# The norms' root factor stays in the PSUM bank of the sums

## The reference

```
def rms_norm(x, w):
    xf = x.astype(jnp.float32)
    y = xf * lax.rsqrt(jnp.mean(xf * xf, axis=-1, keepdims=True) + EPS)
    return (y * w.astype(jnp.float32)).astype(x.dtype)
...
for i in range(DEPTH):
    hn = rms_norm(h, norm_mix_pre[i])
    ...                                   # m = the mixer of layer i, on hn
    h = h + rms_norm(m.astype(h.dtype), norm_mix_post[i])
    hn = rms_norm(h, norm_ffn_pre[i])
    f = swiglu_ffn(hn, ffn_w_gate[i], ffn_w_up[i], ffn_w_down[i])
    h = h + rms_norm(f, norm_ffn_post[i])
return h[:, N_META:]
```

## Time and profile before

| What | before |
|---|---|
| median of 3 runs | 3541.22 us |
| lowest and highest run | 3526.09 and 3548.99 us |
| the profiled execution's own time | 3545.44 us |
| its span | 3543.6 us |
| TensorE busy | 3055.1 us, 86% |
| VectorE busy | 1366.1 us, 39% |
| GpSimd busy | 949.4 us, 27% |
| ScalarE busy | 787.8 us, 22% |

### The profile page before, as it was taken

The page is one execution under the profiler, slowest core; times in us unless marked ns, Lnnn a source line. Parts: engine busy times, 40 slices in busy tenths (PEclk is TensorE's granted clock), DMA queues, the critical chain, the costliest instruction groups (busy, mean ns, idle before and its releaser), DMA issues.

```text
span 3543.6 us, 45716 instructions
## 1 busy us (share of the span) xinstructions
PE 3055.1 (86%) x18053; PEld 2867.9 (81%) x18053; DVE 1366.1 (39%) x2269; ACT 787.8 (22%) x1395; POOL 949.4 (27%) x390
## 2 busy tenths in 40 slices
PE   4999877776769899999999876676898999999996
PEld 3999866664548799999999776455897999999995
DVE  2662255544561532322322424765015323223223
ACT  3221143324561310000000431222114100000002
POOL 2443200000003334443543222000423344435430
PEclk8999998876679999999999986555999999999998
DMA  4122300100002221111111242112212211111101
GB/s 158 66 98 88 126 24 27 39 7 20 34 18 68 97 71 47 48 47 36 55 45 42 76 101 50 37 36 42 92 47 84 68 48 47 47 36 59 47 25 64
DMA packets 138917, 201.04 MB, mean 57 GB/s; under 512 B 32208, under 2 KB 108496, under 8 KB 138320
## 3 DMA queue, kind: packets, MB, share of 16 engines
q1 hardware_dynamic: 54544, 113.99, 10.6%
q10 hardware_dynamic: 84288, 85.84, 7.4%
HBM read 153.20 MB, written 46.60 MB: 56 GB/s over the span
## 4 chain that ended last, share of the span: by engine, by line
issue 33%; PE 33%; DVE 13%; POOL 11%; ACT 6%; DMA 3%; ACTq 1%; POOLq 0%; DVEq 0%; SPq 0%
POOL w_hi L486 8%; PE bank L514 5%; PE bank L515 5%; PE bank L516 5%; POOL w_lo L490 3%; PE bank L568 3%; DVE area L1642 2%; PE bank L729 2%; DMA stage<-wstream 2%; DVE area L1565 2%; PE bank L959 1%; PE bank L960 1%; PE bank L721 1%; DVE area L1650 1%; DVE area L1900 1%
## 5 line engine op out<-in xcount | busy, mean ns | idle before, releaser
L514 PE MATMUL bank<-x_hi,w_hi 128*128 128x344 f32 (+2 forms) x3600 | 1166.7, 324 | 60.4 <-DVE x_lo L1588 34.4
L515 PE MATMUL bank<-x_lo,w_hi 128*128 128x344 f32 (+2 forms) x3600 | 1161.2, 323 | 0.0
L516 PE MATMUL bank<-x_hi,w_lo 128*128 128x344 f32 (+2 forms) x3600 | 1156.9, 321 | 0.0
L486 POOL TENSOR_TENSOR w_hi<-stage,const 128x1024 fp32r<-128x1024 f32 x193 | 474.2, 2457 | 2483.7 <-PE bank L516 2463.9
L514 PEld LDWEIGHTS bank<-x_hi,w_hi 128*128 128x128 f32 x3600 | 683.8, 190 | 67.6 <-DVE x_lo L1588 32.7
L515 PEld LDWEIGHTS bank<-x_lo,w_hi 128*128 128x128 f32 x3600 | 682.9, 190 | 1.9
L516 PEld LDWEIGHTS bank<-x_hi,w_lo 128*128 128x128 f32 x3600 | 683.5, 190 | 0.0
L490 POOL TENSOR_TENSOR w_lo<-stage,w_hi 128x1024 fp32r<-128x1024 f32 x193 | 479.2, 2483 | 15.1
L514 PE MATMUL bank<-act_hi,w_hi 128*128 128x344 f32 (+1 forms) x1056 | 347.3, 329 | 31.9 <-DVE area L1945 24.3
L1932 DVE TENSOR_TENSOR area<-area,bank 128x352 f32<-128x352 f32 (+1 forms) x132 | 68.0, 515 | 758.0 <-ACT area L1368 758.0
L516 PE MATMUL bank<-act_hi,w_lo 128*128 128x344 f32 (+1 forms) x1056 | 341.7, 324 | 0.0
(11 more groups left out here) (217 smaller groups left out, 2876.8 us busy)
## 6 DMA issues: line engine op xcount, KB each, us to landing
stage<-wstream SPq DMA_DIRECT2D x193, 512.0 KB, 3.3
proj<-area ACTq DMA_DIRECT2D x28, 520.0 KB, 2.6
area<-proj ACTq DMA_DIRECT2D x40, 256.0 KB, 4.4
resid<-area ACTq DMA_DIRECT2D x6, 1376.0 KB, 5.7
area<-resid ACTq DMA_DIRECT2D x6, 1376.0 KB, 8.6
area<-proj ACTq DMA_DIRECT2D x12, 520.0 KB, 4.3
area<-xT ACTq DMA_DIRECT2D x4, 1376.0 KB, 8.2
resid<-area ACTq DMA_DIRECT2D x3, 1408.0 KB, 6.2
```

Source lines behind the costliest of these rows:

```text
L486: pool.tensor_tensor(per_block(w_hi[:, slot, :]), per_block(stage[:, h, :]), all_ones, ALU.mult).then_inc(high_split, 1)
L514: mm(out[:, 0:n], w_hi[:, slot, wk], hi[:, xk, a:a + n], start=first, stop=False)
L515: mm(out[:, 0:n], w_hi[:, slot, wk], lo[:, xk, a:a + n], start=False, stop=False)
L516: return mm(out[:, 0:n], w_lo[:, slot, wk], hi[:, xk, a:a + n], start=False, stop=last)
```

## The change

Ln and Exp write their result to bank 7, in place over the sums, and VectorE's products read it there as their second tensor input. Since the bank now holds the factor until the products have read it, the sum of an event no longer waits for the Ln of the event before, but for that event's products: nm_normed if it was a pre, nm_resid (the products and the sum onto the residual) if it was a post. The two waits of ScalarE that kept rs apart are gone, and rs is not used any more. The order of the work on each engine stays.

```
+def norm_before(e):
+    at = e - 1
+    if at < 3:
+        return 0, at, 1
+    if at < 21:
+        return 1 + (at - 3) // 6, (at - 3) % 6 // 2, (at - 3) % 2
+    return 4, at - 21, 0
...
                 e = norm_event(r, c, m)
                 if e:
-                    pe.wait_ge(nm_log, e)
+                    r0, c0, m0 = norm_before(e)
+                    pe.wait_ge(*((nm_normed, 3 * r0 + c0 + 1) if m0 else (nm_resid, 3 * (r0 - 1) + c0 + 1)))
...
-                rs = nv["rs"][m][:, 0:n]
-                if m and 3 * r + c:
-                    act.wait_ge(nm_normed, 3 * r + c)
-                elif not m and 3 * (r - 1) + c:
-                    act.wait_ge(nm_resid, 3 * (r - 1) + c)
                 act.wait_ge(nm_sum, e + 1)
-                A(rs, norm_sums[:, 0:n], ACT.Ln, scale=1.0 / D, bias=eps_col).then_inc(nm_log, 1)
+                A(norm_sums[:, 0:n], norm_sums[:, 0:n], ACT.Ln, scale=1.0 / D, bias=eps_col).then_inc(nm_log, 1)
                 act.wait_ge(nm_log, e + 1)
-                A(rs, rs, ACT.Exp, scale=-0.5).then_inc(nm_root, 1)
+                A(norm_sums[:, 0:n], norm_sums[:, 0:n], ACT.Exp, scale=-0.5).then_inc(nm_root, 1)
...
             def norm_scale(r, c, m):
                 dve.wait_ge(nm_root, norm_event(r, c, m) + 1)
-                return nv["rs"][m][:, 0:CUTS[c][1]]
+                return norm_sums[:, 0:CUTS[c][1]]
```

## The result

The changed kernel takes **3492.11 us** (median of 4 runs, 3489.91 to 3492.68), the kernel before 3539.99 us (4 runs, 3526.09 to 3548.99). The ratio is 0.9867, with a 95% interval of 0.9834 to 0.9900: 47 us or 1.3% faster. I had forecast 3517 us, with 3499 as the lower end of the range. The direction was right, and the gain was twice the forecast (47.9 us by the medians against 24.2).

The account below looks back on a forecast made before the run. TensorE, busy 86% of the span, bounds the kernel through its waits and low clock. Terms -15.7 - 11.2 - 4.2 + 2.8 + 4.1 = -24.2 us, against 3541.22, gave 3517 us; range 3499 to 3540.

Parts of the forecast that it names:

- Part 1: At r=1 and r=3, products reading the bank stop waiting for GpSimd: gains of 15.7, 11.2 and 4.2 us.
- rival A: Products, keeping a weight pointer in SBUF, go on losing to GpSimd and both stretches stay: 3548 us, chance 0.12.
- Rival B: The contest with GpSimd moves to the addition at r=1 and r=3, 8 us given back: 3525 us, chance 0.15.
- Part 2: The sum waits for the products: cost 2.8 us at the start, cut 1, and 4.1 us at r=2, cut 2.
- Part 3: Changed lengths of the products, Ln and Exp, and ScalarE's removed waits: each taken as 0.
- rivals C: Reading the bank is slow, priced at 61 ns for each product: 3523 us, chance 0.08.
- D: More gain: the clock holds at r=3 and r=2, products shrink by 63 ns: 3507 us, chance 0.10.

Follow-up runs that it names:

- P and B: The changed kernel with ScalarE's two waits put back ahead of its wait for the sum, the factor staying in the bank: 3512.09 us, ratio 0.9919.
- W: ScalarE's two waits removed; run alone on the kernel before (kept only at the start, cut 1), factor in SBUF: 3513.46 us, ratio 0.9930.
- P alone: The kernel before with only the sum's wait changed, to the products of the event before: 3544.48 us, ratio 1.0022.
- P and W: The changed kernel with Ln and Exp writing the factor to SBUF again and the products reading it there: 3523.69 us, ratio 0.9969.

## Why the prediction was wrong

**Part 1, the bank read: right in kind and in size.** The products no longer wait for GpSimd, so rival A is out, although each keeps its weight pointer in SBUF. At r = 1 the time from the first post products to the sum of (cut 2, post) fell from 1145.10 to 1219.61 = 74.5 us to 1138.24 to 1196.47 = 58.2: 16.3 us against 15.7 forecast. P and B without W has the same 58.2 (1144.83 to 1203.06). At r = 3, where I had 11.2 + 4.2 = 15.4, the same distance fell from 76.3 (2645.17 to 2721.42) to 57.8 us (2618.66 to 2676.44), 18.5. With P and B alone it is 60.1 (2636.43 to 2696.49), so 16.2 are the bank's and 2.3 W's, since table loads lie in that distance too. Two assumptions were too dark. At r = 1 the addition was to lose 2.2 us to GpSimd and lost none: it takes 3.02 us, and the GpSimd instruction that starts with it takes 5.29. At r = 3 it was to lose 1.5 and lost 1.0 (4.00 us in all), since only 1.1 us of a GpSimd instruction were left. And at r = 3 the clock stayed up. Rival B, the contest moving to the addition, did not come: the longest of the 12 additions now takes 3.995 us against 5.175.

**Part 2, the new wait: right alone, cheaper in company.** Alone it cost what the prediction had, 6.9 us forecast and about 8 measured (2 to 13 by the interval). At its two places it was 3.9 us at r = 2 (4.1 forecast) and, from the first Ln to the last products of r = 0, 3.3 us at the start (2.8 forecast). In the changed kernel the sum at r = 2 waits 2.48 us instead of the 3.97 that it waits with P alone, and ScalarE has loaded its table by the time that the sum ends. The rows of TensorE and then of ScalarE:

```profile
2010.72 5.72 PE L579 MATMUL bank<-area,const 128*128 128x344 f32 x13 [2.48 <-DVE area L1586]
```

```profile
2013.22 1.28 ACT L1040 ACT_TABLE_LOAD   x1
2017.35 0.52 ACT L1040 ACTIVATE bank<-bank,sb_eps 128x344 f32<-128x344 f32 x1 [2.85 <-PE bank L579]
```

Post follows pre by 12.9 us (2006.72 to 2019.66): 2.7 us more than before, not 4.1, though the clock fell as forecast (the whole sum takes 6.59 us). At the start the sum begins at 41.60 us, right behind the products that end at 41.55, and the last products of r = 0 begin at 74.4 us instead of 72.8: 1.6 us late and not 2.8. With ScalarE's two waits put back (P and B) they begin at 77.8 us, so it is W that makes the new wait cheaper.

**Part 3: the step that failed.** "The removed waits of ScalarE were met already: 0." They were met; the runs say nothing against that. What I did not ask is what else stood behind a wait. With two waits ahead of Ln, the one for the sum stood ahead of the table load, and at 19 of the 24 events its 1.28 us could only start when the sum was done. The load is even in my, at 2041.98, where I took it for the moment at which ScalarE comes and put no price on it. Removing the waits, or only swapping them, brings 18 to 20 us in the profiles (ratios 0.9930 and 0.9940), where my sum had 0. That is nearly all of the 25 us between the forecast and the result. The view of the matmuls of line 568 in the kernel before has it in two lines that I did not read closely, those of who waited for them (us in total, times):

```profile
  ACT L1034: 65.5, 16
  ACT area L1034: 21.5, 5
```

The first is the table load, which writes no tile, and it stood 16 times until the sum was done; the second is Ln itself, 5 times, at the five events without a load behind the sum. The expectations multiplied 1.3 us by the number of events on TensorE's path, first nine and later 12 to 15; the later number was fitted to the gain. The traces do not bear it out as a count: a part of the gain is the missed collision at r = 2, cut 0.

The small terms: a product takes 568 ns in the median with its factor in the bank and took 575 to 576 in SBUF, so 0 was close, the 61 to 63 ns of rivals C and D are out, and the rule of the Trainium skill ("VectorE: DVE Perf Modes", the section on the TRN2 errata) of 62 cycles more for a PSUM source does not show here. Ln and Exp, which I bounded but took as 0, became shorter by 26 and 49 ns (548 to 522, and 491 to 442):

```profile
L1040 ACT ACTIVATE bank<-bank,sb_eps 128x344 f32<-128x344 f32 x16 | 8.4, 522 | 35.1 <-PE bank L579 35.0
L1042 ACT ACTIVATE bank<-bank 128x344 f32<-128x344 f32 x16 | 7.1, 442 | 0.2
```

**What stays open.** The untouched stretch between r = 0 and r = 1 varies by 14 us between the first seven profiles, and the runs of the kernel before lie between 3519.87 and 3548.99 us. Which instruction varies was not followed up. P and W (3523.69 us) and W alone (3513.46) differ by 10 us in the medians, while their profiled executions (3512.00 and 3511.72 us) end within 0.3 us of each other; whether that is this stretch too, no trace shows.

## What to carry to other kernels

Where GpSimd works on SBUF beside VectorE, look for VectorE lines whose longest case is several times the median; moving one of two SBUF inputs into a bank took a stretch of 17 us to 4. When a wait is added or removed ahead of an activation, look at where the waits stand in the compiled order: a table load belongs ahead of the wait for the late producer. Here the wait written last stood ahead of the load and the one written first lay on the activation, in either order of the two, and that order decided 18 us. A reuse wait that looks dear alone can be cheap once another step of the same chain is shorter, so price it within the changed chain.

## What the runs showed of the hardware

- A product with one SBUF tensor, a pointer in SBUF and one tensor in a bank (564 to 583 ns in 192 cases, GpSimd working beside some) is not touched by GpSimd; with two SBUF tensors the same product took up to 2770 ns.
- Where VectorE's addition with two SBUF tensors met GpSimd, one of the two waited: at r = 1 the addition took its usual 3.02 us and the GpSimd instruction that started with it 5.29 instead of 2.4; at r = 3 the addition took 4.00.
- ScalarE's table load took 1.28 us each time. Where the wait for the sum stood ahead of it, it began behind the sum (16 times ScalarE stood idle for that before); in the changed kernel it was over before the sum ended at 16 of its 20 loads of Ln's table.
- ScalarE's activations became shorter when the output moved from SBUF to a bank: Ln, whose input was in the bank before too, by 26 ns.
- TensorE's clock was granted at 0.50 after 13 us without work at r = 1 and stayed at 1.00 there once the wait was gone; with it went 2.8 us of a sum's 7.55.
